# Stores of the MLP's partial sums one pair later and apart, and a reciprocal cut in four

## The reference, cut to what matters

```python
D_FF = 4 * D_MODEL          # 4096, D_MODEL = 1024

def trunk(x, mem, p):
    for i in range(DEPTH):                       # 2
        x = x + hybrid_mixer(rmsnorm(x, p["norm_mix"][i]), p, i).astype(x.dtype)
        x = x + memory_cross_attention(rmsnorm(x, p["norm_xattn"][i]), ...)
        hdn = rmsnorm(x, p["norm_mlp"][i]) @ p["w_up"][i]
        x = x + (jnp.square(jax.nn.relu(hdn)) @ p["w_down"][i]).astype(x.dtype)
    return rmsnorm(x, p["norm_final"])
```

## Time and profile before

| | |
|---|---|
| median of 3 runs | 2316.51 us (2315.48 to 2317.64) |
| profiled execution | 2324.39 us, its span 2322.5 us |
| PE busy / PEld busy | 2269.8 us (98%) / 2114.4 us (91%) |
| DVE / ACT / POOL busy | 1611.4 (69%) / 1275.4 (55%) / 443.3 us (19%) |
| mean granted TensorE clock | 0.993 |
| POOL's queue q0 | 135.30 MB, 34.4% of 16 engines |
| SP's queue q1 | 175.19 MB, 23.7% of 16 engines |

### The profile page before, as it was taken

One profiled execution on the slowest core, in us unless ns is written; L12 is line 12 of the kernel. 1 busy time (PEld: TensorE's weight loads), 2 busy tenths in 40 slices (PEclk: granted clock), 3 DMA queues, 4 the chain that ended last, 5 costly groups with the idle time before them and its releaser, 6 DMA issues.

```text
span 2322.5 us, 33654 instructions
## 1 busy us (share of the span) xinstructions
PE 2269.8 (98%) x12336; PEld 2114.4 (91%) x12336; DVE 1611.4 (69%) x2665; ACT 1275.4 (55%) x2616; POOL 443.3 (19%) x512
## 2 busy tenths in 40 slices
PE   8999999999999999999999999999999999999898
PEld 7999679898999999999989995998979999989897
DVE  7988774465587856756678878736656977667566
ACT  5554435555565656656446545445455656656562
POOL 1121002200113222231211110023002122231320
PEclk9999999999999999999999999999999999999999
DMA  5554327842466586687655553288215576775974
GB/s 159 117 110 104 91 87 170 183 106 55 90 169 175 126 180 132 139 184 220 125 120 110 106 126 91 69 178 183 79 46 129 150 189 129 151 168 119 221 198 109
DMA packets 128705, 313.10 MB, mean 135 GB/s; under 512 B 14678, under 2 KB 28246, under 8 KB 128548
## 3 DMA queue, kind: packets, MB, share of 16 engines
q0 software_dynamic: 72128, 135.30, 34.4%
q1 hardware_dynamic: 55844, 175.19, 23.7%
q10 hardware_dynamic: 576, 0.52, 0.1%
HBM read 276.36 MB, written 34.60 MB: 134 GB/s over the span
## 4 chain that ended last, share of the span: by engine, by line
PE 82%; DMA 7%; DVE 6%; ACT 2%; issue 2%; POOL 1%; SPq 0%; DVEq 0%; POOLq 0%; ACTq 0%
PE G L1342 28%; PE G L1861 6%; DMA w_low<-wstream 6%; PE M L1861 6%; PE G L1872 4%; PE M L1872 4%; PE G L1909 3%; PE M L1307 2%; PE M L1305 2%; PE M L1306 2%; PE M L1342 1%; DVE tap L2084 1%; PE M L1571 1%; PE G L1785 1%; PE G L1877 1%
## 5 line engine op out<-in xcount | busy, mean ns | idle before, releaser
L635 POOL DMA_DIRECT2D wlo<-wstream x236 | 209.2, 887 | 1061.4 <-ACT wlo L687 889.7
L648 POOL DMA_DIRECT2D w_low<-wstream x192 | 180.8, 945 | 661.6 <-ACT w_low L1059 661.4
L687 ACT ACTIVATE wlo<-raw 128x512 fp32r<-128x512 f32 x220 | 138.2, 628 | 304.9 <-PE G L1342 229.0
L1342 PE MATMUL G<-A_hi,whi 128*128 128x384 f32 x864 | 294.2, 340 | 9.2 <-DVE A_lo L2044 8.8
L1342 PE MATMUL G<-A_hi,wlo 128*128 128x384 f32 x864 | 290.3, 336 | 0.0
L1342 PE MATMUL G<-A_lo,whi 128*128 128x384 f32 x864 | 285.4, 336 | 0.0
L1070 ACT ACTIVATE whi<-raw 128x384 fp32r<-128x384 f32 (+1 forms) x224 | 128.8, 575 | 120.7 <-DVE raw L2613 77.6
L1070 ACT ACTIVATE whi<-raw_b 128x384 fp32r<-128x384 f32 (+1 forms) x224 | 128.8, 575 | 111.5 <-DVE raw_b L2613 71.8
L1342 PEld LDWEIGHTS G<-A_hi,whi 128*128 128x128 f32 x864 | 163.3, 189 | 13.2 <-issue 11.1
L1342 PEld LDWEIGHTS G<-A_lo,whi 128*128 128x128 f32 x864 | 162.9, 189 | 1.0
L1342 PEld LDWEIGHTS G<-A_hi,wlo 128*128 128x128 f32 x864 | 163.1, 189 | 0.0
(11 more groups left out here) (555 smaller groups left out, 6180.7 us busy)
## 6 DMA issues: line engine op xcount, KB each, us to landing
raw<-wstream SPq DMA_DIRECT2D x172, 512.0 KB, 4.2
wlo<-wstream POOLq DMA_DIRECT2D x236, 256.0 KB, 5.3
w_low<-wstream POOLq DMA_DIRECT2D x96, 256.0 KB, 4.7
w_low<-wstream POOLq DMA_DIRECT2D x96, 192.0 KB, 3.9
down_sum<-staged POOLq DMA_DIRECT2D x48, 384.0 KB, 6.6
raw_b<-wstream SPq DMA_DIRECT2D x32, 512.0 KB, 6.5
raw_b<-wstream SPq DMA_DIRECT2D x32, 384.0 KB, 4.3
raw<-wstream SPq DMA_DIRECT2D x32, 384.0 KB, 4.3
```

Of the source, the lines that this page charges most:

```text
L635: pool.dma_start(low, wstream[stream(L, c)][:, part], accum_op=ALU.add).then_inc(lo_in[c % 2][h], 16)
L648: pool.dma_start(w_low[i][:, 0:n], wstream[w + 2 * f + row][:, col * n:(col + 1) * n], accum_op=ALU.add).then_inc(u_lo[i], 16)
L687: act.activation(wlo[:, s, part], raw[:, s, part], ACT.Copy, scale=-1.0).then_inc(neg_done, 1)
L1342: last = mm(out, w, p[:, k, a:b], start=(k == 0 and w is w_hi and p is parts[0]), stop=(k == KT - 1 and (w is w_lo and only is None or onl ...
```

## The change

Two edits.

1. `down_out` takes one row of a pair. The two stores of down pair f - 2 now stand in the list of pair f: the first between its low transfers 0 and 1, the second between 1 and 2. Waits, sizes and destinations are unchanged.
2. `correction` has seven parts at the steps (4, 0), (4, 2), (5, 0), (5, 1), (5, 2), (6, 1) and (6, 2). The reciprocal is four of 192 columns, the last four parts. The second multiplication comes after pair 4.

```diff
+CORRECTION = ((4, 0), (4, 2), (5, 0), (5, 1), (5, 2), (6, 1), (6, 2))
...
-                def down_out(f):
+                def down_out(f, row):
 
                     r, U = down_row(f), L * FAST + f
-                    if f >= STEP and r == 0:
+                    if f >= STEP and r == 0 and row == 0:
                         for i in range(2):
                             pool.wait_ge(y_out[i], 32 * outputs_before(L, f))
...
                 for f in range(FAST):
                     for i in range(3):
                         pair_low(f, i)
-                    if f and is_down(f - 1):
-                        down_out(f - 1)
+                        if f > 1 and is_down(f - 2) and i < 2:
+                            down_out(f - 2, i)
...
-                        link(dve.reciprocal(rbc[:, :], sq[:, 0:T]))
+                        piece = slice((part - 3) * T // 4, (part - 2) * T // 4)
+                        link(dve.reciprocal(rbc[:, piece], sq[:, piece]))
...
-                        if j in (7 * UPS + 7, 7 * UPS + 8, 7 * UPS + 9, 7 * UPS + 15):
-                            correction((7 * UPS + 7, 7 * UPS + 8, 7 * UPS + 9, 7 * UPS + 15).index(j))
+                        if (f, n) in CORRECTION:
+                            correction(CORRECTION.index((f, n)))
```

More of the change, by code:

```diff
@@ L649, in pair_low @@
                                    accum_op=ALU.add).then_inc(u_lo[i], 16)
-                def down_out(f):
+                def down_out(f, row):
                     r, U = down_row(f), L * FAST + f
-                    if f >= STEP and r == 0:
+                    if f >= STEP and r == 0 and row == 0:
                         for i in range(2):
                             pool.wait_ge(y_out[i], 32 * outputs_before(L, f))
[L657 to L666, removed]
+                    if row == 0:
+                        pool.wait_ge(u_c, 3 * U + 4)
+                    else:
+                        pool.wait_ge(u_c21, L * PAIRS + 4 + f + 1)
+                    if f < STEP:
+                        pool.dma_start(down_sum[L, 2 * r + row], staged[r % 2][row][:, :]).then_inc(y_out[r % 2], 16)
+                    else:
+                        pool.dma_start(down_sum[L, 2 * r + row], staged[r % 2][row][:, :],
+                                       accum_op=ALU.add).then_inc(y_out[r % 2], 16)
                 for f in range(FAST):
```

## The result

The changed kernel takes 2277.61 us (median of 4 runs, 2275.65 to 2279.20), the one before 2315.99 us (4 runs): a ratio of 0.9836, 95% interval 0.9819 to 0.9853, or 38.4 us less. 2274 was forecast, with 2266 to 2298 as the range. The two profiled executions are further apart, 2324.39 and 2278.16 us, by 46.2 us; the prediction's 44.5 was read from the first of them.

A forecast was written before the change was run, and what follows sets the result against it. TensorE was taken to bound the kernel, sometimes waiting for transfers. Stalls 30.1, clock 11.8 and reciprocal 2.6 make 44.5 us off 2324.39, factor 0.981; times 2316.51 gives 2272.2, plus 2 us allowed: 2274, range 2266 to 2298.

The forecast's parts named there:

- The 12 stalls at low transfer 0: TensorE's waits for the first low transfer in both layers' MLPs, behind two adding stores: all go, 30.1 us.
- within 5 us: Sign of being right in the profile after: low transfers 0 land within 5 us of issue, against 8.6 allowed.
- Low transfers 1 and 2 fit: Second and third low transfers, one store directly ahead: 7.2 us against 8.8 and 8.6 allowed; cost 0, bound 2.0 us each place.
- The stores have 9.0 us before VectorE wants their buffer: Second store of a down pair, before VectorE overwrites its buffer two pairs later: 10.8 us before TensorE feels it; cost 0.
- The reload of X: After pair 27: later stores delay the reload and pair 31's raw weights by 0 to 3 us; cost 0, bound 3 us a layer.
- The reciprocal: VectorE, pair 5: 4.95 us whole, quarters about 1.24 us; TensorE's 1.3 us wait in each layer goes, gain 2.6 us.
- The stalls, 30.1 us: TensorE's 12 waits for first low transfers in the two MLPs, all won back: 30.1 us.
- the clock, seven dips, 11.8 us: Granted clock near 0.66 for 5 us at seven of the 12 stalls, 1.7 us each: 11.8 us won back.
- 2 us for small new waits: Allowance over the scaled 2272.2 us for small waits that come up once the large ones are gone: 2 us.
- The DMA engines as the bound: Rival, 14%: full DMA engines in the down pairs make low transfers 1 or 2 late; half the stalls stay, 2293 us.
- The stall that moves: Rival, 6%: the store behind low transfer 0 hits low transfer 1 as hard; only the reciprocal is won, 2314 us.
- The slower case: Rival, 3%: the second store holds VectorE's first sum in third and fourth down pairs, 16 places; 2322 us.

The follow-up runs named there:

- The first edit alone: Changed kernel with its stores moved but the reciprocal whole, as in the kernel before: 2279.78 us, ratio 0.9835 to the kernel before; repeated, 2280.38 us.

## Why the prediction was right, point by point

- *The 12 stalls at low transfer 0 go.* So they did, and for the reason given. The first edit alone gives the gain; in the old order taking most of the stores' data away gives it too, and so does not adding. The flight was mis-sized: 4 to 5 us were forecast, and "within 5 us" was a sign of being right. It was 3.8 at pair 12, but 5.0 to 7.0 in pairs 14, 21 and 28 and up to 7.4 in the down pairs 13, 20 and 27, where the second store of an earlier pair is still under way ahead of it. Against 8.6 allowed this cost nothing.
- *Low transfers 1 and 2 fit, 7.2 us of 8.6.* In the down pairs and the first up pair behind them 8.0 at the longest, against 8.8 allowed. The margin is thin: with the stores side by side, low transfer 1 took 11.3 us. That 7.2 was worked out as half the price of two stores is not borne out as a rule.
- *The stores have 9.0 us before VectorE wants their buffer, 10.8 before TensorE feels it.* 9.2 us in the trace after, no wait. Some five us later it is missed at 11 of 12 places.
- *The reload of X, 0 to 3 us late, cost 0.* ScalarE waited 1.0 us for `raw_b` in layer 1 and 2.0 us in layer 0 (waits of ACT, 1030 to 1080 us):

```profile
ACT w_low L1059 <- DMA raw_b<-wstream: 2.0, 1, 2.0
```

  TensorE did not notice.
- *The reciprocal, quarters of 1.24 us, gain 2.6 us.* The waits went. A quarter takes 2.73 / 2 = 1.37 us (timeline of DVE, 728 to 736 us), two of them cost 0.25 us more than half a whole:

```profile
730.23 2.73 DVE L2671 RECIPROCAL rbc<-sq 128x192 f32<-128x192 f32 x2
733.00 0.56 DVE L2650 TENSOR_TENSOR staged<-p_one,M 128x384 f32<-128x384 f32 x1
```

- *The stalls, 30.1 us, and the clock, seven dips, 11.8 us.* Both terms stood in one profiled execution, and it was 7.9 us above the median. Together they were too large for the runs: 42.5 us below the median were forecast, 38.4 measured. The prediction saw the 7.9 us and only scaled by a factor, which takes almost nothing off; its 2 us for small new waits were not needed, since none came up. Both terms differ between executions. In the profile of the reciprocal alone, with the stores in the old order, 12 stalls of 1 us or more (24.7 us in all, not 30.1) brought three dips in the MLPs, at about 1960, 1987 and 2175 us, not seven (windows over its MLPs; the clock is the third number from the end):

```profile
655.00:1095.00 440.00, 427.99 (x2435) 422.12 (x2435) 315.26 (x572) 276.18 (x580) 113.41 (x132) 1.00 0.73 167
1800.00:2245.00 445.00, 429.14 (x2403) 421.94 (x2402) 314.85 (x572) 276.07 (x579) 113.50 (x133) 0.99 0.72 163
```

  The 33 runs of the kernel before made beside the experiments have a granted clock of 0.993 to 0.997, mostly 0.995; the profiled execution had 0.993. The changed kernel has 0.998 or 0.999. From 0.995 to 0.998 the clock gives back 0.003 x 2316, about 7 us; from 0.993 it is 11.6, the sum's figure. With 24.7 to 30.1 us of stalls and 2.5 of the reciprocal, 7 us of clock make 34 to 40 us, and 38.4 was measured. How the missing 4 us divide between shorter stalls and fewer dips stays open: waits are seen in the profiled executions alone.
- *Rivals.* The DMA engines as the bound fell with the small stores in the new order. The stall that moves was seen in part with the stores together. The slower case came with both stores behind low transfer 2.

Not settled: where the 3.4 us come from that low transfer 0 takes behind two small or two plain stores over one alone. The stores' own 1.3 to 2.1 us on the engines are part of it. With the small stores POOL's own row of that transfer is 1.96 us long, against 0.86 for one alone. SP's loads of raw weights were in flight beside it, and no run takes them away.

## What to carry to other kernels

A transfer with a deadline goes first; one that only frees a buffer can follow, as long as it lands before the buffer is wanted again, so work out both deadlines before choosing the place. Spread such stores: one ahead of an urgent transfer fit here, two did not, and both stores too late was worse than the old place. Adding to DRAM is the dear part of such a store, so price it by a row of its own kind and not by its bytes. And before you carry stalls and clock dips of a profiled execution over to the median, look how far it lies above the other runs: here it had more of both than another profile of the same stores.

## What the hardware showed unexpectedly

- Stalls of 2.1 to 3.5 us on TensorE sometimes bring the granted clock to its lower level for a while and sometimes don't: 7 dips for 12 such stalls in the profiled execution before, 3 for 12 of 1.0 to 2.9 us in that of the reciprocal alone. One of 2.2 us had a dip (842.76 us), one of 2.4 us had none (2064.01 us). In the changed kernel, whose longest wait in the MLPs is 0.6 us, there is none.
- An adding store of 384 KB to DRAM lands in 7.1 us in the median (5.5 to 10.0), a plain one of the same bytes in 4.7 (3.8 to 6.6), in the same order of issue. With the engines full the adding ones moved 157 GB/s, the plain ones 368.
- Behind two stores issued just ahead, a low transfer takes 7.1 us even where these are a sixth in size, against 3.7 alone.
- A reciprocal on VectorE costs 4.95 us for 768 columns and 1.37 for 192: by these two points about 6.2 ns a column (3.58 / 576) and 0.17 us fixed.
